# A convolution and mixture-of-experts block: the gather takes turns with the first expert, and the last expert runs by column blocks beside the closing layer norm

## What is computed

```python
h = layer_norm(ALPHA * h + conformer_conv(h), ln_mix_g, ln_mix_b)
# router: every token gets 2 of 32 experts (of one of 4 groups) and two gates
ffn[tok] = sum over its 2 experts e of gate * ((silu(h @ w_gate[e]) * (h @ w_up[e])) @ w_down[e])
out = layer_norm(ALPHA * h + ffn, ln_ffn_g, ln_ffn_b)
```

## Time and profile before

| | |
|---|---|
| median of 3 runs | 1353.23 us (1352.06 to 1354.21) |
| the profiled execution: its own time | 1354.78 us |
| its span (first to last instruction) | 1353.0 us |
| PE busy | 1226.5 us (91%) |
| DVE / ACT / POOL busy | 438.9 / 249.3 / 275.2 us |
| read from HBM | 462.09 MB |
| mean granted clock of PE | 0.978 |

### The profile page before, as it was taken

One profiled execution on the slowest core, in us unless ns is written; L12 is line 12 of the kernel. 1 busy time (PEld: TensorE's weight loads), 2 busy tenths in 40 slices (PEclk: granted clock), 3 DMA queues, 4 the chain that ended last, 5 costly groups with the idle time before them and its releaser, 6 DMA issues.

```text
span 1353.0 us, 16204 instructions
## 1 busy us (share of the span) xinstructions
PE 1226.5 (91%) x6135; PEld 646.1 (48%) x6135; DVE 438.9 (32%) x880; ACT 249.3 (18%) x316; POOL 275.2 (20%) x119
## 2 busy tenths in 40 slices
PE   6999999999699998999899899979998997999892
PEld 5999996687443432343244234323423432343240
DVE  2899998402811221212022121202211120211206
ACT  4545453432310100010011001000100200010020
POOL 6999996186200000000000000000000000000000
PEclk9999998999899999999999999999999999999996
DMA  9656655156479999999999999999999999999981
GB/s 286 193 167 176 186 178 233 35 194 232 193 296 421 422 421 421 421 421 421 422 422 422 422 422 422 422 422 421 422 421 422 422 422 421 422 422 422 422 338 63
DMA packets 127764, 464.66 MB, mean 343 GB/s; under 512 B 7281, under 2 KB 74865, under 8 KB 75633
## 3 DMA queue, kind: packets, MB, share of 16 engines
q1 hardware_dynamic: 127730, 464.21, 86.3%
HBM read 462.09 MB, written 2.10 MB: 343 GB/s over the span
## 4 chain that ended last, share of the span: by engine, by line
DMA 57%; PE 20%; POOL 13%; issue 4%; DVE 3%; SPq 2%; ACT 1%; POOLq 0%; DVEq 0%; ACTq 0%
DMA ring<-in_wu 56%; POOL ring_r L419 10%; PE ps L1085 10%; PE ps L983 5%; POOL terms L426 1%; PE ps L1123 1%; PE ps L1046 1%; SPq L354 1%; POOL terms L429 1%; PE ps L933 1%; PE ps L1065 1%; DMA ring<-in_w 1%; PE ps L958 1%; DVE stats L682 0%; DVE terms_r L720 0%
## 5 line engine op out<-in xcount | busy, mean ns | idle before, releaser
L1085 PE MATMUL ps<-ring,gain_bias 128*64 128x512 f32 x2048 | 462.4, 603 | 60.7 <-DMA ring<-in_wu 60.2
L1085 PEld LDWEIGHTS ps<-ring,gain_bias 128*64 128x64 f32 x2048 | 156.0, 138 | 362.3 <-issue 361.0
L419 POOL TENSOR_TENSOR ring_r<-ring,ring_r 128x2048 fp32r<-128x2048 f32 x48 | 220.9, 4620 | 59.4 <-ACT ring_r L475 59.4
L1123 PE MATMUL ps<-ring,xT 128*64 128x512 f32 x1024 | 226.8, 595 | 4.6 <-DVE xT L856 4.6
L444 POOL TENSOR_TENSOR rstd<-mv,minus_half 128x1 f32<-128x1 f32 x4 | 2.2, 550 | 1002.1 <-DVE mv L685 1002.1
L851 DVE TENSOR_TENSOR xT<-xT,ps 128x256 f32<-128x256 f32 x32 | 13.5, 421 | 477.0 <-ACT xT L562 477.0
L634 DVE SCALAR_TENSOR_TENSOR ps<-u,par,ps 128x256 f32<-128x256 f32 x384 | 151.8, 482 | 0.0
L912 PE MATMUL ps<-x_hi,ring_r 128*128 128x272 f32 x1024 | 136.3, 290 | 13.3 <-ACT ring_r L475 12.3
L1123 PEld LDWEIGHTS ps<-ring,xT 128*64 128x64 f32 x1024 | 70.7, 137 | 147.1 <-issue 139.3
L912 PEld LDWEIGHTS ps<-x_hi,ring_r 128*128 128x128 f32 x1024 | 132.5, 190 | 13.6 <-ACT ring_r L475 12.3
L1065 PE MATMUL ps<-xT,pickT 128*128 128x512 f32 x256 | 124.4, 619 | 2.2 <-DVE xT L866 2.2
(11 more groups left out here) (138 smaller groups left out, 636.9 us busy)
## 6 DMA issues: line engine op xcount, KB each, us to landing
ring<-in_wg SPq DMA_DIRECT2D x128, 1024.0 KB, 22.7
ring<-in_wu SPq DMA_DIRECT2D x128, 1024.0 KB, 24.8
ring<-in_wd SPq DMA_DIRECT2D x128, 1024.0 KB, 20.4
ring<-in_w SPq DMA_DIRECT2D x48, 1024.0 KB, 6.1
xT<-in_xT SPq DMA_DIRECT2D x2, 1088.0 KB, 8.6
h<-in_x SPq DMA_DIRECT2D x1, 2048.0 KB, 7.6
gain_bias<-in_ln_g SPq DMA_DIRECT2D x2, 1024.0 KB, 7.2
gain_bias<-in_ln_b SPq DMA_DIRECT2D x2, 1024.0 KB, 6.3
```

Source lines behind the costliest of these rows:

```text
L419: nc.gpsimd.tensor_tensor(ring_r[:, lo_slot(c), :], ring[:, raw_slot(c), :], ring_r[:, hi_slot(c), :].bitcast(f32), ALU.subtract).then_inc ...
L1085: mm = nc.tensor.matmul(ps_gu[hh * SLOTS:(hh + 1) * SLOTS, :].rearrange("p (a f) -> p a f", a=2), xgT[:, g * 8 + c0 + c, q, :], ring[:, s: ...
L1123: mm = nc.tensor.matmul(ps_y[g * SLOTS:(g + 1) * SLOTS, nb, :], midT[:, f % 2, (f // 2) * SLOTS:(f // 2 + 1) * SLOTS], ring[:, s, g * 1024 ...
```

## The change

It has two parts, and one thing that goes with them.

- **Start.** PE gathers only four of the eight steps for quad 0 before expert 0; it does steps 4 and 5 after the first pair of chunks, and steps 6 and 7 after the second. The registers are loaded from `quads_i` after quad 0, on PE, ACT and DVE.
- **Last expert.** The last quad is written out (`quad(last, ends=True)`) without the gather for a following one. In its last expert w_down comes in four column blocks of 512 instead of four row blocks, in rows of 2 KB instead of 8 KB. PE works through them as D0 D1 C0 D2 C1 D3 C2 C3, where Dc is the down product of block c (16 instructions of 256 columns) and Cc its combine (two products of 128x512). Ahead of the last expert PE puts h's last 512 columns in PSUM (`prime_end`), so that C3 adds onto them there. DVE adds blocks 0 to 2 and takes their statistics as they come.
- **Closing layer norm.** The statistics of both tiles end together; one power on POOL, one Newton step for both. DVE centres tile 1, ACT multiplies it with the root, POOL adds its bias; DVE does tile 0 alone. ACT copies three blocks of the gain to PSUM first. SP writes 8 blocks of 256 KB, in the order (t, c) below. Gain and bias are loaded as soon as the last pair of gate and up has been used.

```diff
@@ SP
-            sp.wait_ge(freed[UP_END], QUAD * quads)
-            sp.wait_ge(x_sb, 8 * quads + 8)
+            for q in range(QUAD):
+                expert_chunks(QUAD * last + q, E - QUAD + q, ends=(q == QUAD - 1))
+            sp.wait_ge(freed[UP_END], QUAD * last + QUAD)
             sp.dma_start(gain, ...); sp.dma_start(bias, ...)
+            for t, c in ((1, 0), (1, 1), (1, 2), (0, 0), (1, 3), (0, 1), (0, 2), (0, 3)):
+                cols = slice(c * 512, (c + 1) * 512)
+                sp.wait_ge((out_dve, out_pool)[t], c + 1)
+                sp.dma_start(out[t * P:(t + 1) * P, cols], result[:, t, cols]).then_inc(out_s, 16)
@@ SP, expert_chunks
+                    if kind == "down" and ends:
+                        sp.dma_start(ring[:, s, :].rearrange("p (f n) -> p f n", f=4),
+                                     wd_end[e, :, :, a * 512:(a + 1) * 512]).then_inc(arrived[s], 16)
@@ POOL
+            inverse_root(1 + TT, rstd[:, :], mv[:, :, 1])
+            pool.wait_ge(bias2_s, 16)
+            for c in range(4):
+                pool.wait_ge(scaled_r, c + 1)
+                nc.gpsimd.tensor_tensor(result[:, 1, cols], result[:, 1, cols], bias[:, cols], ALU.add
+                                        ).then_inc(out_pool, 1)
@@ ACT
-            quads = load_quads(act)          # now behind quad(0)
+            act.wait_ge(add_ps, 16 * last + 8)
+            for c in range(4):
+                act.wait_ge(end_ps, c + 1)
+                nc.scalar.activation(y[SLOTS:P, c * 512:c * 512 + 256], ps_y[0:SLOTS, c % 2, 0:256], ACT.Copy
+                                     ).then_inc(end_y[0], 1)
+                if c == 1:
+                    act.wait_ge(gain2_s, 16)
+                    for b in range(2):
+                        nc.scalar.activation(ps_gain[:, b, :], gain[:, b * 512:(b + 1) * 512], ACT.Copy
+                                             ).then_inc(gain_ps, 1)
...
+            act.wait_ge(rstd_2, 1)
+            for c in range(4):
+                act.wait_ge(centred_g, c + 1)
+                nc.scalar.activation(part, part, ACT.Copy, scale=rstd[:, 1:2]).then_inc(scaled_r, 1)
@@ DVE
+            def end_rows(c):
+                dve.wait_ge(end_ps, c + 1)
+                nc.vector.tensor_copy(y[SLOTS:P, c * 512 + 256:(c + 1) * 512], ps_y[SLOTS:P, c % 2, 0:256]
+                                      ).then_inc(end_y[1], 1)
+            def end_add(c):
+                for t in range(TT):
+                    dve.wait_ge(add_ps, adds + 2 * c + t + 1)
+                    if c < 3: nc.vector.tensor_tensor(h[:, t, cols], h[:, t, cols], ps_add[:, t, :], ALU.add)
+                for t in range(TT):
+                    ins = nc.vector.bn_stats(stats[:, t, c, :], h[:, t, cols] if c < 3 else ps_end[:, t, :])
+            end_rows(0); end_rows(1); end_add(0); end_rows(2); end_add(1); end_rows(3); end_add(2); end_add(3)
+            # 2 bn_aggr, 1 tensor_scalar -> var_ready
+            # centre(1, 0), centre(1, 1), Newton step for both tiles, centre(1, 2), centre(1, 3)
+            for c in range(5):
+                if c < 4:
+                    centre(0, c).then_inc(centred_0, 1)
+                if c > 0:
+                    nc.vector.scalar_tensor_tensor(out=result[:, 0, cols], in0=ps[:, SCALED_BANK[c - 1], :],
+                                                   scalar=rstd[:, 0:1], in1=bias[:, cols], ...)
@@ PE
-            gather(0, range(8))
-            quads = load_quads(pe)
-            last_pair = load_last_pair(pe)
+            gather(0, range(0, 4))
             quad(0)
+            quads = load_quads(pe)
+            last = load_last(pe)
+            last_adds = load_last_adds(pe)
@@ PE, quad
+                        if n_is_first(n) and j < 4:
+                            gather(0, range(4 + j, 6 + j))
...
-                    if q == QUAD - 1:
+                    if q == QUAD - 1 and not ends:
                         gather(i + 1, range(0, 4))
...
+                    if q == QUAD - 1 and ends:
+                        pe.wait_ge(pT_sb, pair + 1)
+                        end_down(0, n)
+                        for c in range(1, 4):
+                            end_down(c, n)
+                            end_combine(c - 1, 16 * last + 8)
+                        end_combine(3, 16 * last + 8)
+                        break
```

More of the change, by code:

```diff
@@ L590, in inverse_root @@
             def inverse_root(root, var, tmp):
+                tmp = tmp[:, 0:1]
                 n_root[0] += 1
@@ L877, in _ @@
-            dve.wait_ge(all_added, 1)
-            dve.wait_ge(gain2_s, 16)
-            dve.wait_ge(bias2_s, 16)
[L882 to L885, removed]
+            quad(last, ends=True)
+            adds = 16 * last + 8
+            def end_rows(c):
+                dve.wait_ge(end_ps, c + 1)
+                nc.vector.tensor_copy(y[SLOTS:P, c * 512 + 256:(c + 1) * 512], ps_y[SLOTS:P, c % 2, 0:256]
+                                      ).then_inc(end_y[1], 1)
@@ new lines, in _, with centre @@
+            end_rows(0)
+            end_rows(1)
+            end_add(0)
+            end_rows(2)
+            end_add(1)
+            end_rows(3)
+            end_add(2)
+            done(end_add(3))
+            for t in range(TT):
+                ins = nc.vector.bn_aggr(mv[:, t, :], stats[:, t, :, :].rearrange("p c s -> p (c s)"))
+            done(ins)
+            nc.vector.tensor_scalar(mv[:, :, 1], mv[:, :, 1], LN_EPS, None, ALU.add).then_inc(var_ready, 1)
+            def centre(t, c):
+                cols = slice(c * 512, (c + 1) * 512)
+                src, by = (h[:, t, cols], ps_gain[:, c, :]) if c < 3 else (ps_end[:, t, :], gain[:, cols])
+                return nc.vector.scalar_tensor_tensor(
+                    out=ps[:, SCALED_BANK[c], :] if t == 0 else result[:, 1, cols], in0=src,
+                    scalar=mv[:, t, 0:1], in1=by, op0=ALU.subtract, op1=ALU.mult)
@@ new lines, in end_combine @@
+            def end_combine(c, adds):
+                pe.wait_ge(end_y[0], c + 1)
+                pe.wait_ge(end_y[1], c + 1)
+                for t in range(TT):
+                    if c < 3:
+                        pe.wait_ge(added, adds + 2 * max(c - 1, 0) + (t + 1 if c else 0))
+                    nc.tensor.matmul(ps_add[:, t, :] if c < 3 else ps_end[:, t, :], pickT[:, t, :],
+                                     y[:, c * 512:(c + 1) * 512], start=(c < 3), stop=True).then_inc(add_ps, 1)
@@ L1069, in quad @@
+            def quad(i, ends=False):
+                adds = 16 * i - 8 if not ends else last_adds
                 for q in range(QUAD):
@@ L1072, in quad @@
                     combines = q % 2 == 0 and not (q == 0 and isinstance(i, int))
+                    if q == QUAD - 1 and ends:
+                        prime_end(16 * last + 8)
                     wait(pe, act_done, n)
```

191 lines of the change are left out of this document (124 added, 67 removed).

## The result

The changed kernel takes 1331.59 us (median of 4 runs, 1331.04 to 1334.4) against 1353.42 us: a ratio of 0.984 (95% interval 0.9827 to 0.9852), 21.8 us less. 1329.1 was forecast. The profiled execution took 1331.04 us, its span 1329.2 us against 1353.0.

The account below looks back on a forecast made before the run. The expert stage was taken as bound by its weight transfers at 422 GB/s, so only the refills' start and what follows the last w_up count. Start 5.8 plus end 18.3 gave 24.1 us off 1353.23: 1329.1 us, range 1325 to 1334.

Parts of the forecast that it names:

- The stream's start: At expert 0, the first slots are given back for refill at 374.2 against 380.57, 6.3 us sooner; 5.8 us gained overall.
- The holes: Gaps in the weight stream between the first refills, from gather steps between pairs of chunks: 0.3 and 0.4 us.
- The end: From the last w_up to the span's end: 35.3 us against 53.6, a gain of 18.3 us.
- `prime_end` and the last pair: Around the last w_up wait: two added products mostly covered by PE's wait, 0.5 us remaining; last pair of chunks 3.65 us.
- to D0: From the last pair to the first down product: 1.96 us as in expert 0, plus 0.42 for the `pickT` copy.
- D and C: Last expert's alternating down and combine products on PE: 7.0 and 6.8 us, 13.8 in all, PE not held up by DVE.
- DVE's part: Closing norm behind C3: remaining statistics, centring, Newton step and tile 0's eight operations, 11.4 us in sum.
- the outputs: After the last operation, three 256 KB blocks leave within a microsecond: 3.4 us, plus 0.2 for SP's order.
- Late column chunks: Rival: last w_down's 2 KB rows move at 269 GB/s, C2 and all behind it 2.7 us late; 1331.8 us, chance 0.12.
- A lower clock in the tail: Rival: PE runs at 0.70 of 2.4 GHz for the 13.8 us of tail products, adding 5.9 us; 1335.0 us, chance 0.08.
- POOL and DVE: Rival: the two engines slow each other in the closing norm, 2.3 us at the end; 1331.4 us, chance 0.08.
- A thin start of 2.8: Rival: holes restart the stream each time, so the start gives only PE's own 2.8 us; 1332.1 us, chance 0.07.

Follow-up runs that it names:

- the second set: The changed kernel measured once more, unaltered, on the chip of three follow-up runs as their reference: 1333.37 us, ratio 0.9847 to the kernel before.
- the halves of the start: Kernel before with only ACT's register load moved behind quad 0: 1352.62 us; kernel before with gather turns and PE's and DVE's loads moved, ACT's not: 1353.07 us.
- the two queues: The changed kernel with tile 1's four output transfers issued by ACT and tile 0's by SP: 1333.49 us, ratio 0.9853.
- the start alone: The kernel before with only the start changed, gather in turns with expert 0 and registers loaded behind quad 0: 1350.09 us, ratio 0.9968.
- the kernel that makes them do so: The changed kernel with DVE's centring reading the gain in SBUF instead of PSUM: 1335.09 us, ratio 0.9851.

## Why the prediction was right

The span was forecast at 1328.9 and came out at 1329.2; this is partly luck, since 2.7 of its us came from ahead of the change. The medians are the fairer comparison: 24.1 us were forecast, 21.8 measured (20.7 in the second set). Point by point:

- **The stream's start.** "6.3 us sooner" for the first refill: 6.30. Right, with its two causes, as the halves of the start show. **The holes**, taken as 0.3 and 0.4 us, were mis-sized: two gather steps and a pair need 5.70 us (2.12 + 3.58), not 5.35 (1.9 + 3.45), since each switch between them costs PE 0.1 to 0.2. (The sum's 3.45 is also not the 13.95 / 4 that it is said to be, which is 3.49; the refills of the kernel before stood 3.43 apart.) The holes are then 0.7 each, and 1.58 us were lost instead of 0.5. The term of 5.8 measured 4.7.
- **The handover into the last quad** was missing from the sum: 0.92 us. I had priced the registers and jumps at nothing because transfers cover them. They do cover the visible stall, as the kernel without the optional loop shows; but the written-out quad loses about a microsecond of the stream, in part with the code that it fetches.
- **The end**, 18.3 forecast, 17.3 measured. `prime_end` and the last pair 0.6 (0.5); to D0 2.27 (2.4); D and C 14.9, from 1299.40 to 1314.3 (13.8); DVE's part 10.6 (11.4); the outputs 4.3 (3.6: not SP's order, as the two queues show, but the transfers). The errors leave 1.0 us. The largest is D and C, and most of it is C's price: the prediction took 0.86 us a product from the gate and up products, but a combine product takes 0.91 to 0.96 us wherever it stands (8 instructions, four products, in 3.63 to 3.82 us in the changed kernel's chain, 16 in 7.71 in the old tail at full clock). The other 0.4 is D in pieces of 256 columns, 1.84 to 1.88 us each instead of 1.75. Of the 17.3, 1.5 is the old combine's low clock, which no term of the new end had to earn.
- **The rivals.** Late column chunks: no, 385 GB/s and hidden. A lower clock in the tail: no, the clock was 1.00 from 1290 to 1312. POOL and DVE: they don't hold each other up, and the kernel that makes them do so costs 1.2 us. A thin start of 2.8: not by its mechanism, since the holes cost 1.6 us and did not eat the 6.3; but the time of the start alone (2.6 to 6.1 us) does not exclude it.

Without the convolution's share the change gains 21.1 us in that pair of profiles and 21.0 in the second profile of the changed kernel (0.81 + 6.32 - 1.49 - 1.09 + 17.25 = 21.8, the first term being what lies ahead of the gather). So 24.1 was 3 us too much, in the direction of all three mis-sized terms: the stream's holes (1.1), the last quad (0.9), the end (1.0).

**Open**: what costs the stream the rest of the 0.6 to 1.5 us between experts 27 and 30, beyond the 0.45 or less that goes with the fetched code; and why the convolution's second product and the clock in the gather differ from one execution to the next.

## What to carry to other kernels

Where a stream of transfers bounds a kernel, cut the trace at the stream's own events (first refill, the waits on it) and compare lengths, not times: a microsecond of idle queue was not made up here, and a noisy stage ahead no longer hides it. Interleave work ahead of the first refill so that the operand that each piece needs was finished one piece earlier, and count the switches. An exposed tail on one engine is worth spreading over the others until the output transfers are the limit.

## What the runs showed of the hardware that was not expected

- A jump past a loop's code of four experts stops PE for 2.5 us, and PE then runs at a granted clock of 0.66 for the next 5 us. With the code removed the stop is gone, and the clock of 0.66 comes some 60 us later, behind a wait of 3.12 us.
- The code of the last quad is fetched over the DMA engines that carry the weights: 6 or 7 packets in 90 us went with 420 GB/s for the weights instead of 422.
- Alternating gather steps with pairs of gate and up costs PE about 0.1 to 0.2 us a switch, at full clock (2.12 us for two steps against 1.9, 3.58 for a pair against 3.43).
- Two holes of 0.7 us in a full stream of transfers cost it 1.6 us, three of 1.5 us cost 5.8.
- The clock of one and the same gather differs from execution to execution: 1.00, or 0.66 to 0.89 in a stretch of 5 us, with a stall in it or without; first refills of the same instructions came at 7.66 or at 9.16 us.
- The same products of the convolution took from 71.3 to 75.1 us with no change to them, and 71.33 or 73.66 us in two executions of the changed kernel.
